# Two-layer decoder trunk: the layer's end by channel halves, zero products through the norms, moving blocks handed on one by one

## The reference

```python
def reference(x, c, ...):
    c_act = jax.nn.silu(c)
    for i in range(DEPTH):
        mod = c_act @ w_mod[i] + b_mod[i]
        sh1, sc1, g1, sh2, sc2, g2 = jnp.split(mod, N_MOD, axis=-1)
        h = modulate(rmsnorm(x, norm1_g[i]), sh1, sc1)
        y = short_conv_mixer(h, ...) if i == 0 else pool_mixer(h, ...)
        x = x + g1[:, None, :] * y
        h = modulate(rmsnorm(x, norm2_g[i]), sh2, sc2)
        x = x + g2[:, None, :] * peer_ffn(h, ...)
    return rmsnorm(x, final_g)
```

## Time and profile before

| | |
|---|---|
| median of 3 runs | 1914.95 us (1914.13 to 1916.62) |
| profiled execution, device time | 1915.88 us |
| its span (first to last instruction) | 1914.1 us |
| mean granted TensorE clock | 0.985 |
| TensorE products busy | 1864.7 us (97%) |
| VectorE busy | 1525.1 us (80%) |
| ScalarE busy | 860.3 us (45%) |
| mean DMA rate | 194 GB/s |

### The profile page before, as it was taken

How to read it: one execution, slowest core, us unless ns; L and a number is a source line. 1 busy time by engine, 2 the same in 40 slices (tenths; PEclk the granted TensorE clock), 3 DMA queues, 4 the chain that set the end, 5 groups by cost and what they waited for, 6 DMA issues and landing times.

```text
span 1914.1 us, 39829 instructions
## 1 busy us (share of the span) xinstructions
PE 1864.7 (97%) x14820; PEld 1729.5 (90%) x14820; DVE 1525.1 (80%) x2634; ACT 860.3 (45%) x1281; POOL 4.0 (0%) x8
## 2 busy tenths in 40 slices
PE   5989999999999999999999999999999999999998
PEld 5989999999999888888889899999999988888887
DVE  7986698888888888788868668889788888885554
ACT  3334444454334444454544544444433444444543
POOL 0000000000000000000000000000000000000000
PEclk9998999999999999999989999999999999999998
DMA  7976455555454555698835655555445455555552
GB/s 298 333 280 227 145 185 179 185 169 167 159 159 142 170 175 170 235 333 318 316 112 168 243 168 172 183 186 180 164 151 163 138 172 164 174 194 191 191 192 88
DMA packets 101339, 370.38 MB, mean 194 GB/s; under 512 B 11168, under 2 KB 11552, under 8 KB 100640
## 3 DMA queue, kind: packets, MB, share of 16 engines
q1 hardware_dynamic: 100848, 367.43, 57.0%
q10 hardware_dynamic: 432, 2.23, 0.3%
HBM read 366.47 MB, written 3.15 MB: 193 GB/s over the span
## 4 chain that ended last, share of the span: by engine, by line
PE 91%; DVE 6%; DMA 2%; issue 1%; ACT 1%; SPq 0%; DVEq 0%; ACTq 0%
PE ps L1093 46%; PE acc L1242 37%; PE gp L1191 5%; DVE acts L576 2%; DVE low L557 1%; PE gp L1053 1%; PE gp L1180 1%; DMA raw<-conv_in 1%; DMA acts<-w_mod 1%; PE gp L1064 0%; DVE acts L629 0%; DMA raw<-conv_out 0%; DVE acts L934 0%; ACT high L371 0%; PE gp L1080 0%
## 5 line engine op out<-in xcount | busy, mean ns | idle before, releaser
L557 DVE TENSOR_TENSOR low<-raw,high 128x1024 fp32r<-128x1024 f32 x596 | 727.6, 1222 | 325.9 <-ACT high L371 323.6
L371 ACT ACTIVATE high<-raw 128x1024 fp32r<-128x1024 f32 x593 | 626.9, 1057 | 483.4 <-PE acc L1242 384.8
L1093 PE MATMUL ps<-mov_h,high 128*128 128x256 f32 x2704 | 778.8, 288 | 15.2 <-DVE mov_l L635 7.2
L1093 PE MATMUL ps<-mov_l,high 128*128 128x256 f32 x2704 | 770.3, 285 | 0.0
L1093 PE MATMUL ps<-mov_h,low 128*128 128x256 f32 x2704 | 770.0, 285 | 0.0
L1093 PEld LDWEIGHTS ps<-mov_h,high 128*128 128x128 f32 x2704 | 523.7, 194 | 18.7 <-issue 13.9
L1093 PEld LDWEIGHTS ps<-mov_l,high 128*128 128x128 f32 x2704 | 524.8, 194 | 0.0
L1093 PEld LDWEIGHTS ps<-mov_h,low 128*128 128x128 f32 x2704 | 524.2, 194 | 0.0
L1242 PE MATMUL acc<-high,mov_h 128*128 128x512 f32 x1024 | 403.4, 394 | 1.0 <-DVE mov_l L991 0.8
L1242 PE MATMUL acc<-high,mov_l 128*128 128x512 f32 x1024 | 399.6, 390 | 0.0
L1242 PE MATMUL acc<-low,mov_h 128*128 128x512 f32 x1024 | 399.5, 390 | 0.0
(11 more groups left out here) (108 smaller groups left out, 743.1 us busy)
## 6 DMA issues: line engine op xcount, KB each, us to landing
raw<-up SPq DMA_DIRECT2D x256, 512.0 KB, 3.3
raw<-down SPq DMA_DIRECT2D x256, 512.0 KB, 3.9
acts<-w_mod SPq DMA_DIRECT2D x84, 512.0 KB, 5.3
raw<-query SPq DMA_DIRECT2D x32, 512.0 KB, 3.5
raw<-conv_in SPq DMA_DIRECT2D x24, 512.0 KB, 6.9
acts<-w_mod SPq DMA_DIRECT2D x6, 1024.0 KB, 15.4
raw<-conv_out SPq DMA_DIRECT2D x8, 512.0 KB, 7.3
raw<-pool_in SPq DMA_DIRECT2D x8, 512.0 KB, 4.4
```

Source lines behind the costliest of these rows:

```text
L371: nc.scalar.activation(flat(high[s]), tile_row(s), ACT.Copy).then_inc(high_ready, 1)
L557: nc.vector.tensor_tensor(flat(low[n % RING]), tile_row(n % RING), flat(high[n % RING]).bitcast(F32), ALU.subtract).then_inc(low_ready, 1)
L1093: ins = nc.tensor.matmul(dst, w[s][:, c], m[:, mv], start=(first and n == 0), stop=(last and n == 2), skip_group_check=skip)
```

## The change

- **conv_in and pool_in hand their moving blocks on one by one.** In the last tile of these stages each channel chunk's third product raises `freed`; ScalarE's `split_z` waits for its chunk alone. VectorE splits chunks 0 to 6 (conv) or 0 to 5 (pool) ahead of the last tile's evacuation, and the rest behind it. In pool_group the splits stand between the tiles.
- **Norms.** VectorE scales all eight chunks and then writes all eight mov_l (but for k = 0). TensorE runs the first two tiles behind norms 1, 2 and 3 together: first all products with mov_h, which wait for mov_h alone, then those with mov_l (`first_two`).
- **Zeros through norms.** `keep_warm` issues 12 products of zeros (bf16, 128 columns) ahead of `spread` (k = 1 to 4) and 13 behind it (k = 1, 2, 3).
- **Layer ends by channel halves.** The last four down tiles run banks 0 and 1 first, then banks 2 and 3. The first half is turned back behind the first of the second passes, and added and squared beside the others. The next stage's first low parts move from the tiles before into this stretch, as do ScalarE's roundings.
- **Modulation sums** of blocks 0 and 1 of layer 1 stand apart, behind the sixth and the fifth tile from the end.
- **Turns** use TensorE's transpose in the place of a product with the identity.
- `run` writes the first four and the last four tiles out and loops over the rest.

```diff
@@ ScalarE @@
-            def split_z(n_products, ready):
-                act.wait_ge(product, n_products + RING)
+            def split_z(free, ready):
                 for c in range(DC):
+                    act.wait_ge(*free(c))
                     act.wait_ge(*ready(c))
                     nc.scalar.activation(mov_h[:, c], Z[:, c], ACT.Copy).then_inc(mh_done, 1)
...
-                    split_z(AT[0, "conv_out"], lambda c: (evac_dve, 2 + 3 * (c + 1)))
+                    split_z(lambda c: (freed, c + 1), lambda c: (evac_dve, 2 + 3 * (c + 1)))
...
-                    split_z(AT[1, "pool_group"], lambda c: (z_ready, c + 1))
+                    split_z(lambda c: (freed, DC + c + 1), lambda c: (z_ready, c + 1))
                     only_round(AT[1, "pool_group"], 4)
-                    split_z(AT[1, "pool_out"], lambda c: (evac_dve, 2 + 32 + 8 + c // 2 + 1))
+                    split_z(lambda c: (product, AT[1, "pool_group"] + c // 2 + 1 + RING),
+                            lambda c: (evac_dve, 2 + 32 + 8 + c // 2 + 1))
...
+                evac(0)
+                squares(0)
+                if layer == 0:
+                    ahead(0, last, 1)
+                    ahead(0, last, 2)
+                evac(2)
+                if layer == 0:
+                    ahead(0, last, 3)
+                squares(DC // 2)
             norm(4)
@@ VectorE @@
+                else:
+                    for c in range(DC):
+                        scaled(c)
+                    if k < 4:
+                        for c in range(DC):
+                            rest(c)
...
-                        p = bank(n0, 3 * j + 2)
+                        slot(n0 + 3 * j + 2)
+                        if j == DC - 1:
+                            split_z(0, DC - 1)
+                        dve.wait_ge(product, n0 + 3 * j + 3 + RING)
                         need(three)
-                        nc.vector.tensor_tensor(Z[:, j], p, cv[:, 2], ALU.mult).then_inc(evac_dve, 1)
+                        nc.vector.tensor_tensor(Z[:, j], ps[:, (3 * j + 2) % 2, 0:T], cv[:, 2],
+                                                ALU.mult).then_inc(evac_dve, 1)
+                        if j == DC - 1:
+                            split_z(DC - 1)
                         use_mtile(4, j, (j + 1) * 16, 1)
...
+                            slot(n0 + j)
+                            if j == DC - 1:
+                                split_z(0, DC - 2)
+                            dve.wait_ge(product, n0 + j + 1 + RING)
...
-                    split_z()
+                        if j:
+                            split_z(2 * j - 2, 2 * j)
+                    split_z(DC - 2)
...
-                for j in range(HALF):
+                for j in range(HALF - AHEAD):
...
+                dve.wait_ge(acc_done, 3 * layer + 2)
+                evac(1)
                 dve.wait_ge(reloaded, 16 * (layer + 1))
+                add_to_x(0)
+                slot(n0 + KEYS - 3)
+                slot(n0 + KEYS - 2)
+                dve.wait_ge(product, n0 + KEYS + RING)
+                evac(3)
+                add_to_x(DC // 2)
+                slot(n0 + KEYS - 1)
@@ TensorE @@
+            def keep_warm(n):
+                for _ in range(n):
+                    nc.tensor.matmul(acc[:, 3, 0:P], zeros[:], zeros[:], start=True, stop=True)
...
+            def first_two(layer, name, evac, evac0):
+                pe.wait_ge(low_ready, AT[layer, name] + 2)
+                pe.wait_ge(evac, evac0 + 2)
+                def one(s, w, m, c, first, last):
+                    return nc.tensor.matmul(ps[:, s, 0:T], w[s][:, c], m[:, c], start=first, stop=last)
+                for c in range(DC):
+                    pe.wait_ge(mh_done, moved[0] * DC + c + 1)
+                    for s in range(2):
+                        one(s, high, mov_h, c, c == 0, False)
+                        one(s, low, mov_h, c, False, False)
+                lag = DC // 2
+                for c in range(DC + lag):
+                    if c < DC:
+                        moving(c)
+                        ins = one(0, high, mov_l, c, False, c == DC - 1)
+                        if c == DC - 1:
+                            ins.then_inc(product, 1)
+                    if c >= lag:
+                        ins = one(1, high, mov_l, c - lag, False, c - lag == DC - 1)
+                ins.then_inc(product, 1)
...
+                    if last:
+                        ins.then_inc(freed, 1)
+                if last:
+                    pe.wait_ge(freed, (layer + 1) * DC)
+                    pe.sem_inc(product, 1)
...
+                keep_warm(12)
                 spread(2 * layer + 1)
-                run(layer, "query", 16, evac_act, out_act)
+                keep_warm(13)
+                run(layer, "query", 16, evac_act, out_act, True)
...
-                        ins = nc.tensor.matmul(dst[:, tc * P:(tc + 1) * P], src[:, tc * P:(tc + 1) * P], eye,
-                                               start=True, stop=True)
+                        ins = nc.tensor.transpose(dst[:, tc * P:(tc + 1) * P], src[:, tc * P:(tc + 1) * P], eye)
...
+                        for s in range(RING):
+                            down_tile(HALF // RING - 2, s)
+                            if s >= 2:
+                                next_sum(s - 2)
+                        for s in range(RING):
+                            arrived(HALF // RING - 1, s)
+                            down_banks(s, (0, 1), s == RING - 1)
...
+                for s in range(RING):
+                    down_banks(s, (2, 3), s == RING - 1).then_inc(product, 1)
+                    if s == 0:
+                        turn_back(0)
+                square_sums(2 * layer + 2, 0, 2)
+                turn_back(DC // 2)
+                square_sums(2 * layer + 2, 2, DC)
+                keep_warm(12)
             spread(4)
```

More of the change, by code:

```diff
@@ L530, in _, with evac @@
                         load_table(ACT.Sqrt)
-                    for s in range(RING):
-                        if last + s + AHEAD < TILES:
+                    ahead(0, last, 0)
+                    weight(first + HALF - 1, RING - 1)
+                    if half == 0:
+                        for s in range(1, RING):
                             ahead(0, last, s)
-                        if s + AHEAD < RING:
-                            if last + s + AHEAD >= TILES:
-                                act.wait_ge(product, last + s + AHEAD + 1)
-                            weight(first + HALF - RING + s + AHEAD, (s + AHEAD) % RING)
-                for b in (0, 2):
+                def evac(b):
                     act.wait_ge(acc_done, 3 * layer + b + 1)
@@ L541, in _, with squares @@
                                          ).then_inc(acc_out_act, 1)
+                def squares(c0):
+                    for c in range(c0, c0 + DC // 2):
+                        act.wait_ge(x_ready, layer * DC + c + 1)
+                        square(c)
+                evac(0)
[7 more added lines that the diff above has]
+                squares(DC // 2)
             norm(4)
@@ L1104, in project, with run @@
                         moving(c)
[L1105 to L1111 removed]
+                    ins = three(ps[:, s % 2, 0:T], s % RING, c, c, c == 0, c == DC - 1)
+                    if last:
+                        ins.then_inc(freed, 1)
+                if last:
+                    pe.wait_ge(freed, (layer + 1) * DC)
+                    pe.sem_inc(product, 1)
+                else:
+                    ins.then_inc(product, 1)
+            def run(layer, name, tiles, evac, evac0, behind_norm=False):
+                if behind_norm:
+                    first_two(layer, name, evac, evac0)
+                for s in range(2 if behind_norm else 0, RING):
+                    project(layer, name, 0, s, evac, evac0)
+                n = tiles // RING - 2
+                if n:
+                    with pe.Fori(0, n) as i:
+                        for s in range(RING):
+                            project(layer, name, i, RING + s, evac, evac0)
+                for s in range(tiles - RING, tiles):
+                    project(layer, name, 0, s, evac, evac0, name in ("conv_in", "pool_in") and s == tiles - 1)
                 if name != "query":
```

176 lines of the change are left out of this document (87 added, 89 removed).

## The result

| | before | changed | changed, a second time |
|---|---|---|---|
| median | 1914.97 us (1914.13 to 1916.62, 4 runs) | 1904.57 us (1901.44 to 1905.35, 4 runs) | 1901.77 us (1900.09 to 1903.38, 6 runs) |
| ratio to before, beside it | | 0.9943 [0.9928, 0.9958] | 0.9931 [0.9917, 0.9946] |
| profiled span | 1914.1 us | 1903.0 us | 1900.1 us |

The change makes the kernel faster by 0.4 to 0.8%. The forecast was 1904.3. The second time is the same kernel among the last experiments, where the kernel before took 1915.85 (11 runs): one kernel's runs spread over 2.5 to 7 us, and two medians of the changed kernel differ by 3. So no part of this change, 1 to 3 us each, can be priced by whole times. I read the parts in the traces, as distances between fixed points of the same program.

What follows compares the result with a forecast made beforehand. TensorE carries 91% of the chain and the change touches only the seams where the chain leaves it. The terms sum to 10.6, taking 1915.9 to 1905.3 for a profiled run, 1904.3 for the median; range 1900 to 1911.

Steps and rivals of the forecast that it cites:

- conv_in to conv_out: Between these stages, seven of eight splits move ahead of the gate product and add_mod; first mov_l 1.64 earlier, gain 1.6.
- the sign that I had named: At the start of conv_out: its first product would come 3.2 after the last conv_in product.
- Norms: First two tiles behind norms end 7.5 after the first scaled block; gains 2.2, 0.9 and 2.4 for norms 1, 2, 3.
- Modulation sums: End of layer 0: two groups of 16 between full tiles keep the following tile at full speed; gain 3.4.
- Halves with transposes: Ends of layers, two channel halves with transposes for turns: minus 0.6 in layer 0, gain 0.7 in layer 1.
- Pool stage: Earlier splits on VectorE shorten nothing and add waits: first residual 1.3 later, bounds 0 and minus 2.8.
- Turned numbers: L1213's 12 records become six, 0.67 saved twice: gain 1.3, bounds 0 and 2.0.
- A (transposes give nothing): Turns at layer ends and turned numbers: as many passes or a lower clock; gain 5.8, 1909.1, chance 0.17.
- B (the clock holds through norms and ends): Norms and layer ends: spread takes 0.72, sums 0.105 a record; 1900.5, chance 0.12.
- C (the first two tiles give nothing): Behind norms, ScalarE's table load and evacuations come last; pool's stalls in full; gain 4.5, 1910.5, together 0.12.
- D (slower, the clock falls in the last four tiles): Layer ends and first two tiles: sums apart and transposes bring the clock down; 1922, chance 0.06.
- E (the gain is swallowed in front of "up"): In front of "up": a wait, such as a late query tile, swallows early starts; no change, chance 0.03.

Runs made afterwards that it cites:

- experiment 8: 36 products of zeros put between conv_in's last tile and conv_out, against the changed kernel: 1901.94 us, ratio 0.9935.
- experiment 2: The changed kernel without the zero products at the norms: 1905.08 us, ratio 0.9939.
- experiment 3: The changed kernel with the first two tiles behind a norm one after the other, scaled and rest interleaved on VectorE again: 1906.63 us, ratio 0.9955.
- experiment 11: The changed kernel with both layers' ends whole instead of in halves; transposes, modulation sums' places and zeros kept: 1901.0 us, ratio 0.993.
- experiment 6: The changed kernel with the pool stage's two splits behind the last tile of their products again: 1902.09 us, ratio 0.9929.
- experiment 1: The changed kernel with its turns as products with the identity again instead of transposes: 1905.13 us, ratio 0.9949.

## Why the prediction was right, step by step

The sum was 10.6; the profiled spans differ by 11.1, and in the second profile by 14.0.

1. **conv_in to conv_out**, predicted 1.6: 1.67, from the start of ScalarE's rounding to the first product (3.07 to 3.21 in all thirteen profiles, 4.83 before). Another 1.0 of A is that this rounding began earlier, when its DMA had landed: at 109.04 instead of 110.06. Over the twelve runs A varies from 109.97 to 112.67 and the rounding from 106.8 to 109.5, always earlier than in the one profile of the kernel before; whether the change has a part in that is not shown. For the same reason the sign that I had named, 3.2 from the last conv_in product to the first of conv_out, read 2.46 and 3.08 (1.5 to 3.2 in all): the first product hangs on the rounding, not on TensorE's end of conv_in. And one step of the working was wrong. I had TensorE reach the eighth block near 117.7, at 5.04 a tile, with the add_mod done before the modulation sum needs it; the sum began 4.4 after the first product and waited for the add_mod. It cost nothing where the clock was down, and went with a fall behind the tile where it was not (experiment 8): B gave 0.7 back in the first profile and gained 0.3 in the second.
2. **Norms**, predicted 2.2 behind norm 1, 0.9 behind norm 2 and 2.4 behind norm 3. Norm 1: C 2.7 shorter (1.9 the second time). Norm 3: G 2.0 shorter both times. Norm 2, from the last token sum to the copy of tile 1 (1006.91 and 998.77): 0.5, and 0.8. The two tiles end 7.4 to 8.2 after the first scaled block, predicted 7.5. Experiments 2 and 3 show that this needed both the order and the zeros; what the zeros hold up (spread ends 2.16 after the last token sum of norm 1, and 1.67 in experiment 2) is near the 0.4 that I charged; their worth I had not counted at all, since I assumed full speed in the first two tiles.
3. **Modulation sums**, predicted 3.4. To the last down product D became 2.99 shorter; with the inserted transposes (0.87) taken off and the turned numbers (0.68) put aside, 3.2. The size is right, and so is the reason, 32 in a row, with one correction: the fall behind them is likely, not certain (three traces of four).
4. **Halves with transposes**, predicted minus 0.6 and plus 0.7. From the last down product to the last token sum, with the inserted 0.87: layer 0 8.4 instead of 7.5, minus 0.9 (plus 0.4 the second time); layer 1 6.1 instead of 7.6, plus 1.5 both times. The wait that I had named (low parts ahead of the evacuation of bank 3) is the one in the chain. Where the step fell short is layer 1: I took 0.7 off for the clock, which came down only in the last of the sums. What the clock takes varies by more than the step's size: the 24 token sums took 2.6 to 4.7 in layer 0 and 2.6 to 3.7 in layer 1 over the profiles. And the step priced halves and transposes as one; apart and at equal clock, the gain is the transposes' alone (experiment 11).
5. **Pool stage**, predicted minus 1.3, bounds 0 and minus 2.8: the first residual came 1.85 and 1.7 later. The stalls are the three I had named (0.54, 0.41, 1.33) and 0.45 and 0.28 behind them; I had set too much against them for pool_out's early start. But F, behind the first residual, is 0.4 to 0.5 shorter, and experiment 6 shows that this belongs to the same edit: it brings F back to 22.27. With it the stage cost 1.4 and 1.2.
6. **Turned numbers**, predicted 1.3: six records of 0.11 less in each layer, 0.66 instead of 1.34, together 1.4.

So the number was right with the terms that carry it: the six steps add up to 10.7 by the first profile and 11.7 by the second, against 10.6. Steps 2 and 4 were off by 0.3 to 0.8 and by 0.5 to 1.8 with opposite signs. What no step foresaw, the earlier rounding (1.0 and 1.8) and B (minus 0.7 and plus 0.3) above all, came to 0.4 in the first profile and 2.3 in the second; that it nearly cancelled in the first is luck. That the median fell on 1904.6 and not on 1901.8 is luck as well: the range, 1900 to 1911, holds both.

**The rivals.** A (transposes give nothing): out by the records, 8 of 0.11 a turn. The rule of the Trainium skill, page "TensorE: Matmul & The Clock Gate", Part 4, that transposes don't count as activity for the clock gate, is neither shown nor refuted: the sums behind products took 2.59 both times, those behind transposes mostly 3.3 to 4.7, but 2.59 as well in five of 22 (experiment 1). The Terms table on that page of the Trainium skill calls the mode four times as fast for FP32; here it was twice as fast, one record of 0.11 for two. B (the clock holds through norms and ends): it did in no profile throughout. C (the first two tiles give nothing): out by experiment 3. D (slower, the clock falls in the last four tiles): the window there, 967 to 979 us, reads 1.00. Something of it came true, in 1.5 us, only where the sums were one group again. E (the gain is swallowed in front of "up"): C and G reach into "up" and are shorter.

## What to carry to other kernels

When a VectorE or ScalarE queue feeds the end of a stage, look at what stands ahead of the last evacuation: the roundings and low parts for the next stage cost 0.9 us there, more than the 0.5 that the halves' overlap buys by the records. Splitting a stage's end in two halves paid nothing here, once the turns were short. And price parts of 1 to 2 us in a kernel of 1900 by distances between fixed points of the trace, with the changed kernel measured a second time; medians of four to six runs moved by 3 us for the same code.

## What the runs showed of the hardware

- A 128 x 128 f32 transpose is one record of 0.11 us, a product with the identity two.
- Products of zeros in a norm bring TensorE's clock back sooner (it was 0.50 from 146 to 148 us in spite of them, and 1.00 from 150 on; the 48 products took 6.14 instead of 8.37). Ahead of conv_out they did not hold it reliably (B 31.93 once, 35.02 once, with the same 36 zeros).
- One-column products at full clock take 0.105 us a record (16 in 1.68), at half of it 0.2 (24 in 4.71 with the clock at 0.51). In groups of 16 between full tiles they never lowered the clock (ten profiles); 32 in a row did in three of four.
- Eight transposes between down tiles did not lower it either: the 18 records behind them took 4.09 to 4.10 in all 22 cases.
- The place where the clock falls moves between executions of the same kernel: D differs by 1.3, B by 1.1 and C by 0.8 between the two profiles of the changed kernel.
